# Spreading three output products over more slots of a gather-paced decoder trunk

## The reference

```python
def hybrid_attention(...):
    ...
    return o @ w_out                       # (256, 1024) x (1024, 1024)

def conformer_conv(hn, ...):
    ...
    u = jax.nn.silu(layer_norm(u, ln_g, ln_b))
    return u @ w_out + b_out               # (256, 1024) x (1024, 1024) + bias

def peer_ffn(hn, w_q, subkeys, u_tab, v_tab):
    ...                                    # scores, top 16 of 128 twice, top 16 of 256
    u = u_tab[idx]
    act = jax.nn.gelu(jnp.einsum('td,thkd->thk', xc, u), approximate=False)
    v = v_tab[idx]
    return jnp.einsum('thk,thkd->td', (g * act).astype(v_tab.dtype), v)

for layer in range(2):
    h = h + mix(rms_norm(h))
    h = h + peer_ffn(rms_norm(h), ...)
return rms_norm(h)
```

## Time and profile before

| | before |
|---|---|
| median of 3 runs | 1546.85 us (1544.73 to 1546.88) |
| the profiled execution | 1552.11 us |
| its span | 1550.1 us |
| DVE busy | 1088.1 us (70%) |
| PE busy | 1038.0 us (67%) |
| POOL busy | 597.4 us (39%) |
| data moved | 610.77 MB, mean 394 GB/s |

### The profile page before, as it was taken

How to read it: one execution, slowest core, us unless ns; L and a number is a source line. 1 busy time by engine, 2 the same in 40 slices (tenths; PEclk the granted TensorE clock), 3 DMA queues, 4 the chain that set the end, 5 groups by cost and what they waited for, 6 DMA issues and landing times.

```text
span 1550.1 us, 20954 instructions
## 1 busy us (share of the span) xinstructions
PE 1038.0 (67%) x6788; PEld 525.2 (34%) x6788; DVE 1088.1 (70%) x2931; ACT 616.1 (40%) x1855; POOL 597.4 (39%) x516
## 2 busy tenths in 40 slices
PE   7998876777666678675866678576677644444543
PEld 3644442332334345332344355233244301101100
DVE  4446668777435779999655679599775676766784
ACT  2313446542233435555343435345434533333321
POOL 0014435453233445554333344244344344444441
PEclk9999887668778788776877789567788855556555
DMA  9549999999999999999999999999999999999996
GB/s 395 186 146 393 410 376 420 418 394 399 421 401 416 416 419 414 409 418 411 397 381 407 418 412 419 419 420 408 396 414 383 406 419 419 420 419 420 420 420 282
DMA packets 97145, 610.77 MB, mean 394 GB/s; under 512 B 11046, under 2 KB 18598, under 8 KB 28300
## 3 DMA queue, kind: packets, MB, share of 16 engines
q0 software_dynamic: 73728, 536.90, 84.5%
q1 hardware_dynamic: 22492, 72.28, 12.1%
q10 hardware_dynamic: 816, 0.25, 0.1%
HBM read 608.34 MB, written 1.05 MB: 393 GB/s over the span
## 4 chain that ended last, share of the span: by engine, by line
DMA 38%; PE 22%; DVE 21%; issue 12%; ACT 6%; POOL 2%; DVEq 0%; POOLq 0%; SPq 0%; ACTq 0%
DMA ring<-table_dram,idx 32%; PE bank L635 8%; DVE ring L1691 8%; PE ypsum L635 5%; PE qpsum L635 5%; DMA head<-heads_dram 3%; DVE arena L1579 2%; POOL ring L628 2%; ACT L1108 2%; PE spsum L635 1%; DMA arena<-heads_dram 1%; DMA arena<-c_out_dram 1%; ACT ring L1108 1%; DVE topi L1625 1%; ACT wts L1108 1%
## 5 line engine op out<-in xcount | busy, mean ns | idle before, releaser
L628 POOL DMA_INDIRECT ring<-table_dram,idx x512 | 597.2, 1166 | 930.5 <-PE ypsum L635 669.4
L1691 DVE CUSTOM_DVE_ANT_0 ring<-xns,ring 128x1024 f32<-128x1024 f32 x512 | 622.8, 1223 | 320.4 <-DMA ring<-table_dram,idx 316.4
L635 PE MATMUL ypsum<-ring,wts 128*32 128x256 f32 x4096 | 412.5, 498 | 430.0 <-ACT wts L1108 429.3
L1108 ACT ACTIVATE gel<-dot 128x1 f32<-128x1 f32 x512 | 103.0, 201 | 734.0 <-DVE dot L1691 732.9
L635 PEld LDWEIGHTS ypsum<-ring,wts 128*32 128x32 f32 x4096 | 99.5, 124 | 672.1 <-ACT wts L1108 613.8
L1108 ACT ACTIVATE wts<-gident,gel 128x32 f32<-128x32 f32 x512 | 164.6, 321 | 17.0 <-ACT gel L1108 0.2
L635 PE MATMUL qpsum<-head,hT 128*128 128x256 f32 (+1 forms) x324 | 97.9, 464 | 26.6 <-DMA head<-heads_dram 23.1
L1108 ACT ACT_TABLE_LOAD x84 | 107.8, 1283 | 8.3 <-PE bank L640 6.8
L1579 DVE SCALAR_TENSOR_TENSOR arena<-arena,cols 128x128 f32<-128x128 f32 x300 | 88.4, 346 | 0.7
L635 PEld LDWEIGHTS qpsum<-head,hT 128*128 128x128 f32 (+1 forms) x324 | 71.1, 226 | 49.1 <-issue 19.3
L635 PE MATMUL qpsum<-arena 128*128 128x128 f32 x372 | 83.7, 361 | 0.0
(11 more groups left out here) (191 smaller groups left out, 1011.4 us busy)
## 6 DMA issues: line engine op xcount, KB each, us to landing
head<-heads_dram SPq DMA_DIRECT2D x28, 512.0 KB, 8.9
arena<-heads_dram SPq DMA_DIRECT2D x34, 256.0 KB, 7.1
ring<-table_dram,idx POOLq DMA_INDIRECT x512, 12.6
arena<-c_in_dram SPq DMA_DIRECT2D x4, 2048.0 KB, 16.3
arena<-heads_dram SPq DMA_DIRECT2D x7, 1152.0 KB, 25.3
ring<-w_in_dram SPq DMA_DIRECT2D x3, 2048.0 KB, 18.6
arena<-c_out_dram SPq DMA_DIRECT2D x6, 1024.0 KB, 7.9
arena<-w_out_dram SPq DMA_DIRECT2D x1, 4096.0 KB, 37.6
```

Of the source, the lines that this page charges most:

```text
L628: pool.indirect_dma_start(out=row(b), out_offset=None, in_=table[:, :], in_offset=bass.IndirectOffsetOnAxis(ap=idx[R % 2][:, k:k + 1], axi ...
L635: return nc.tensor.matmul(o_, l, r, start=start, stop=stop, **kw)
L1108: return nc.scalar.activation(out_, in_, func, **kw)
L1691: V.tensor_tensor_reduce(out=u, in0=xnr[G % 2], in1=u, scale=1.0, scalar=0.0, op0=ALU.mult, op1=ALU.add, accum_out=dot[:, k:k + 1]).then_i ...
```

## The change

The same instructions of PE, in other slots, and a few steps of ACT and DVE with them:

- `mix_out` takes two `k` a slot over slots 85 to 92 (first half done in 88, second in 92) where it took four in 87 to 90. For that `turn_outputs` moves from 84 to 82 on PE and from 86 to 84 on ACT. DVE adds at 90 and 94 (before 91 and 93).
- `conv_out`'s first half takes two `k` a slot in 86 to 89 (before four in 85 and 86). Its second half takes four in 91 and two each in 92 and 93 (before four in 90 and 91). DVE adds at 91 and 95 (before 89 and 94). ACT's silu stays at 85.
- The wait for the second 1 MB of `cout` stands before `k` = 4 as before; the releases of `cout` go with the steps that they belong to.

```diff
-            def gemm(j, lhs, rhs, width, half=None):
-                bank = banks[bank_no(j)] if half == 1 else bank_of(pe, j)
+            def gemm(j, lhs, rhs, width, ks=None):
                 n = len(lhs)
-                for k in range(n // 2 if half == 1 else 0, n // 2 if half == 0 else n):
+                ks = ks or range(n)
+                bank = bank_of(pe, j) if ks[0] == 0 else banks[bank_no(j)]
+                for k in ks:
                     last = mm(bank[:, 0:width], lhs[k], rhs[k], k == 0, k == n - 1)
-                if half != 0:
+                if ks[-1] == n - 1:
                     last.then_inc(bank_full[bank_no(j)], 1)
+            def quarter(i):
+                return range(i * KD // 4, (i + 1) * KD // 4)
...
-            def conv_out(t, i, half):
-                if half == 0 and i == 0:
+            def conv_out(t, i, ks):
+                if ks[0] == 0 and i == 0:
                     emptied(pe, CONV_AT[t] + J_Z)
                     emptied(pe, CONV_AT[t] + J_Z + 1)
...
+                if ks[0] == 0:
+                    pe.wait_ge(cout_a_in, 16 * (t + i + 1))
+                if ks[0] == KD // 2:
+                    pe.wait_ge(cout_b_in, 16 * (t + i + 1))
+                for k in ks:
                     last = mm(bank[:, :], hT_[:, k, :], cout[:, k, :], k == 0, False)
-                if half == 0:
+                if ks[-1] == KD // 2 - 1:
                     last.then_inc(cout_taken, 1)
-                else:
+                if ks[-1] == KD - 1:
                     pe.wait_ge(cbias_in, 16 * (t + 1))
...
# PE, beside_attention
-                if s == 84:
+                if s == 82:
                     turn_outputs(1)
-                if s in (87, 88, 89, 90):
-                    mix_out(1, (s - 87) // 2, (s - 87) % 2)
+                if 85 <= s < 93:
+                    mix_out(1, (s - 85) // 4, quarter((s - 85) % 4))
...
# PE, beside_conv
-                if s in (85, 86):
-                    conv_out(t, 0, s - 85)
-                if s in (90, 91):
-                    conv_out(t, 1, s - 90)
+                if 86 <= s < 90:
+                    conv_out(t, 0, quarter(s - 86))
+                if s == 91:
+                    conv_out(t, 1, range(KD // 2))
+                if s in (92, 93):
+                    conv_out(t, 1, quarter(s - 90))
...
# ACT, beside_attention
-                if s == 86:
+                if s == 84:
                     turn_outputs(1)
...
# DVE, beside_attention and beside_conv
-                if s in (91, 93):
-                    mix_out(1, (s - 91) // 2)
+                if s in (90, 94):
+                    mix_out(1, (s - 90) // 4)
...
-                if s == 89:
+                if s == 91:
                     conv_out(t, 0)
-                if s == 94:
+                if s == 95:
                     conv_out(t, 1)
```

More of the change, by code:

```diff
@@ L800, in turn_outputs, with mix_out @@
                 turn_over(MIX_AT[t] + J_OT2, o)
-            def mix_out(t, i, half=None):
-                if i == 0 and half != 1:
+            def mix_out(t, i, ks):
+                if i == 0 and ks[0] == 0:
                     emptied(pe, MIX_AT[t] + J_OT2)
@@ L807, in mix_out @@
                 gemm(MIX_AT[t] + J_W + i, [hT_[:, k, :] for k in range(KD)],
-                     [wout[:, k, i * CHUNK:(i + 1) * CHUNK] for k in range(KD)], CHUNK, half)
+                     [wout[:, k, i * CHUNK:(i + 1) * CHUNK] for k in range(KD)], CHUNK, ks)
             def glu(t, i, g):
@@ L836, in tap @@
                 last.then_inc(tap_used if i < len(PE_TAPS) - 1 else bank_full[bank_no(TAPS_JOB[t])], 1)
-            def conv_out(t, i, half):
-                if half == 0 and i == 0:
+            def conv_out(t, i, ks):
+                if ks[0] == 0 and i == 0:
                     emptied(pe, CONV_AT[t] + J_Z)
                     emptied(pe, CONV_AT[t] + J_Z + 1)
-                pe.wait_ge(cout_b_in if half else cout_a_in, 16 * (t + i + 1))
                 j, n = CONV_AT[t] + J_CW + i, out_half(t, i) * CHUNK
-                bank = bank_of(pe, j) if half == 0 else banks[bank_no(j)]
-                for k in range(half * KD // 2, (half + 1) * KD // 2):
+                bank = bank_of(pe, j) if ks[0] == 0 else banks[bank_no(j)]
+                if ks[0] == 0:
[3 more added lines that the diff above has]
+                for k in ks:
                     last = mm(bank[:, :], hT_[:, k, :], cout[:, k, :], k == 0, False)
-                if half == 0:
+                if ks[-1] == KD // 2 - 1:
                     last.then_inc(cout_taken, 1)
-                else:
+                if ks[-1] == KD - 1:
                     pe.wait_ge(cbias_in, 16 * (t + 1))
```

## The result

The changed kernel takes 1553.83 us (median of 7 runs, 1550.22 to 1555.78), the kernel before in the same comparison 1546.88 (7 runs, 1544.73 to 1550.03). The ratio is 1.0037, 95% interval 1.0023 to 1.0051: slower by 5.7 us (3.6 to 7.9). The profiled execution took 1554.37 us, with a span of 1552.5 us, 2.4 us more than that of before. That is less than 5.7 because the profiled execution of before was itself slow: 1552.11 us, 5.2 above the median of its seven runs. The forecast was 1544.9, a gain of 2.0, and the range ended at 1550.5: the time lies outside the range, and it moved the other way.

The account below looks back on a forecast made before the run. The prediction took the DMA engines to pace the slots, with gains only where they lack requests. Attention -1.7, phase 1 -0.3 and phase 2 0 made -2.0 us, from 1546.85 to 1544.9, range 1540.8 to 1550.5.

Parts of the forecast that it names:

- The attention's term: Phase 0, slots 85 to 92: dip closes, norm and `c_in` loads come earlier; gain 1.7 us, between 1.1 and 2.3.
- What bounds the kernel: Whole kernel: DMA engines pace the slots; filling the dips of phases 0, 1 and 2 gives at most 5.7 us.
- The walk: PE's forecast timeline from `add_slot` 85 or 86 on, adding up times of `k`, `add_slot`, bias and waits.
- Convolution, first half: Phase 1, slots 86 to 89: product starts 2.9 us later, ends 3.9 later; earlier gathers fill the 2.0 us dip.
- The second half's wait: Phase 1, slots 91 and 92: PE waits 0.7 us for the first MB of `cout`, 1.5 for the second.
- The clock: PE from the first quarter on: hardly a gap in a slot of 2.5 us, so the clock stays up.
- My fourth rival: PE's clock falls between quarters, 8.8 us a tile before cover; +18, 1565 us; chance 0.03.
- Who pays: Phase 1, gather 103 issued 3.6 us late, partly covered by the queue: repayment 0 to 3.4 us, middle 1.7.
- The second one: Late norm gets through in both convolution tiles, from slot 92's `cout` wait to place 96: +5.4, 1552.2 us; chance 0.13.
- the first rival: All dips in phases 0, 1 and 2 close and nothing is repaid: 1541.2 us; chance 0.20.
- The third: DMA engines lack speed beside a `cout` load, so dips stay and phase 0's advance is cancelled: 1546.9 us; chance 0.15.

Follow-up runs that it names:

- run 1: Kernel before with only the attention's part of the change, convolution in its old slots: ratio 0.9989 to before, -1.7 us.
- run 2: Kernel before with only the convolution's part of the change, attention as before: ratio 1.0067 to before, +10.4 us.
- run 7: Kernel before with the attention's part of the change, convolution in old slots, `cout` loaded once and never again (other output): ratio 0.9984 to before.
- run 4: Kernel before with only the convolution's second half moved (91, 92, 93, addition at 95): ratio 1.0000 to before.
- run 3: Kernel before with only the convolution's first half moved (two `k` each in 86 to 89, addition at 91): ratio 1.0063 to before, +9.7 us.
- run 9: Changed kernel with `cout` loaded in four pieces of 0.5 MB, each when its two `k` are done: ratio 1.0009 to before.
- run 10: Changed kernel with `cout` in four pieces and the convolution at two `k` in each of 86 to 93: ratio 1.0004 to before.
- run 12: Changed kernel with `cout` in four pieces, convolution two `k` a slot in 85 to 88 and 90 to 93, additions at 90 and 95: ratio 0.9983 to before.
- run 11: Kernel before with the attention's part of the change, convolution in old slots, `cout` in four pieces: ratio 0.9986 to before.
- run 5: Kernel before with the convolution's first half one slot later, four `k` each in 86 and 87, not spread: ratio 1.0018 to before, +2.8 us.
- run 6: Kernel before with the convolution's first half spread, two `k` each in 85 to 88, not started later: ratio 1.0032 to before, +5.0 us.
- run 8: Changed kernel with `cout` loaded once and never again (other output): ratio 0.9965 to before.

## Why the prediction was wrong, step by step

The attention's term held. The step that failed is the convolution's: filled dips of 2.0 and 1.8 us, paid back by a delay of some 3.6 us behind a wait for `cout` of 1.5 us, net 0.3 us of gain in phase 1 and 0 in phase 2. Measured, the convolution's part costs 7.4 us (changed kernel against run 1) to 10.4 (run 2 against before), with waits of 3.63 to 4.91 us in slot 92 in three of the four tiles and of 2.20 for the first MB in the fourth.

- **What bounds the kernel.** Right over most of the span, wrong where the change acts. I read the dips as time that the DMA engines could get back. Run 7 shows that bytes taken away there, in the old slots, give 0.8 us (error about 2), not 10: the dip is PE's, and its depth in GB/s says how much other traffic happened to fill it.
- **Attention.** The term of -1.7 us measured -1.7 us in run 1. The interval, -3.4 to -0.2, can't tell 1.7 from the 1.1 and 2.3 between which I had chosen it, so the exact hit is luck. The stretches say -2.6 (mean with, less mean without), of which 1.1 is taken back by slot 80 of phase 1. The walk's order held: places back every 2.5 us, the dip gone, `c_in` issued with the addition. It was 1.7 us too long (24.4 us from `add_slot` 85 to the last quarter; measured from 351.40 to 374.13, 22.7), since the clock rose in the second quarter and not the third.
- **Convolution, first half.** The walk was right: from `add_slot` 86 to the end of the bias 748.1 - 734.65 = 13.4 us, measured 730.64 to 744.31, 13.7. Weights behind silu came as written, and the first quarter took 3.78 us where the walk had 3.4.
- **The second half's wait is the term that was mis-sized.** I took 7.9 us for a load of `cout`, from a trace where it ran beside a starved gather queue, and with it a wait of 1.5 us (by the walk's own numbers PE is there at 754.3 and not 754.6, so 1.8). With the queue filled, which was the aim, it took 10.1 us and the wait was 4.30. The median from issue to landing over the six `cout` loads rose from 7.9 to 9.8 us. The same step filled the dip and slowed the load that PE was about to need; I counted the first only. The Trainium skill (DMA: Bandwidth & Descriptors, Queues, rings and completion order) says that each DMA engine takes turns between the queues it has work for; a load that takes longer beside a filled gather queue fits this, 10.1 against 7.9 us, though no run here shows the turns themselves.
- **The clock.** The half clock before a product stands in before's window from 730 to 735, not in those of the earlier trace rows that I named for it. My fourth rival had it fall between quarters. It didn't there, but it fell in the 4.30 us of waiting: 3.78 and 2.51 us for two quarters in place of 1.98 each, 2.3 us more. The Trainium skill (TensorE: Matmul & The Clock Gate, Why this matters for your kernels) warns of idle gaps between bursts of matmuls, which bring half clock back. The trace agrees for the wait, and shows no such gap at the `add_slot`s between quarters. The half ended 5.1 us later than in the walk (761.6; `add_slot` 86 starts 4.0 us earlier in this profile, so 757.6 on its time, and measured 762.7): the second MB was there 2.4 us later (754.50 against 752.1), and what follows it took 2.7 longer, almost all of it by the clock.
- **Who pays.** I tested the cover at one gather, 103, and for a delay of 3.6 us. POOL was held already at gather 100 (issued at 760.13, by the walk 755.1 on this profile's time), and five gathers in a row went out into a nearly empty queue. The new dip is 6.3 us in those three windows against the 0 to 3.4 of my repayment, and 3.5 in phase 2 against 0 to 3.4.
- **The rivals.** The second one comes nearest. It had the place right (second MB, slot 92) and the sum about right, +5.4 against +5.7. Part of that is luck: it has 3.6 and 3.5 us for two late norms, while the profile has +4.2 and +1.4, and in phase 2 the longer wait was for the first MB. Its chain ran through `peer_start` to place 96; but POOL was held at gather 100 already, which hangs on the `add_slot` of 93, one quarter behind the wait and before the norm, and run 4 shows that the late norm is harmless alone. Its condition was put wrong too. I argued against it by the waits of dots 104 to 108 in before; but those slots had to be reached with a filled ring, and the ring was empty by 100. It had 0.13 and slower in all 0.17. Of the first rival the filled dips came true, in full in phases 0 and 2 and for less than half in phase 1, but what was repaid came to more. The third, that the dips stay, did not come true in phases 0 and 2.

## What to carry to other kernels

Before a consumer is spread out to feed a queue better, list which loads are released by its progress: they start later, and they share the engines with the traffic that now runs better, so their old latency doesn't hold. A dip in GB/s can be won back only if the bytes are what the following slots wait for; take bytes away in an experiment before counting it. And cost a wait on an in-order engine with its clock behind it and with every buffer release that stands in its queue.

## What the runs showed of the hardware

- A 1 MB load that shares the DMA engines with gathers of 8 KB rows took 7.9 us from issue until PE used it when gathers were scarce (before, phase 1), and 10.1 (phase 1 of the changed kernel) and again 1131.55 - 1121.47 = 10.1 us (run 2, phase 2) when they were plenty. The median landing of the six `cout` loads is 7.0 to 7.9 us in before and runs 1 and 4, and 9.5 to 9.8 in the changed kernel and runs 2 and 3. Pieces of 0.5 MB, asked for one behind the other, were no quicker: 11.2, 10.1 and 10.6 us in runs 9, 10 and 12, and 8.8 in the old slots (run 11).
- PE kept 2.4 GHz through quarters of 1.98 us with `add_slot`s of 0.64 between them, and through waits of 1.15 to 1.28 us (runs 9 and 10, phase 1). It was at 1.2 GHz behind waits of 4.30 us (changed kernel) and 4.91 (run 2), and in runs 5 and 6 also behind waits of 1.64 to 2.18.
- Moving 4.2 MB less in stretches where one engine held the buffers changed the time by 0.8 us (run 7 against run 1, error about 2), where 420 GB/s would give 10. In the new slots the same bytes, with the wait for them, were worth 11.1 us (run 8 against the changed kernel).
